# One of two feed-forward PSUM slots handed over bank by bank, a weight split moved behind the third residual addition, and a modulation step moved between two pieces

## The reference, cut to what matters

```python
def dwconv(x, w, b, left):
    K, L = w.shape[0], x.shape[1]
    xp = jnp.pad(x, ((0, 0), (left, K - 1 - left), (0, 0)))
    y = b + w[0] * xp[:, 0:L]
    for k in range(1, K):
        y = y + w[k] * xp[:, k:k + L]
    return y

def conv_ffn(z, w_up, conv_w, conv_b, w_down):
    u = dwconv(z @ w_up, conv_w, conv_b, FFN_CONV // 2)      # FFN_CONV = 3
    g, v = jnp.split(u, 2, axis=-1)
    return (jax.nn.silu(g) * v) @ w_down

# in each layer, for the latent and (in layer 0) the context tokens
mods = jnp.split((silu_c @ mod_w[l] + mod_b[l])[:, None, :], 6, axis=-1)
zl = modulate(rmsnorm(xl, norm2_g[l]), mods[3], mods[4])
xl = xl + mods[5] * conv_ffn(zl, ffn_w_up[l], ffn_conv_w[l], ffn_conv_b[l], ffn_w_down[l])
```

## Time and profile before

| | us |
|---|---|
| median of 3 runs | 3413.1 |
| lowest and highest | 3412.96, 3415.61 |
| the profiled execution's own time | 3416.35 |
| its span, first to last instruction | 3414.8 |
| TensorE matmuls busy | 3175.5 (93%) |
| VectorE busy | 1546.9 (45%) |
| ScalarE busy | 1020.6 (30%) |
| GpSimd busy | 310.6 (9%) |
| granted TensorE clock, mean over the span | 0.967 |

### The profile page before, as it was taken

One profiled execution on the slowest core, in us unless ns is written; L12 is line 12 of the kernel. 1 busy time (PEld: TensorE's weight loads), 2 busy tenths in 40 slices (PEclk: granted clock), 3 DMA queues, 4 the chain that ended last, 5 costly groups with the idle time before them and its releaser, 6 DMA issues. The chain is left out here.

```text
span 3414.8 us, 41073 instructions
## 1 busy us (share of the span) xinstructions
PE 3175.5 (93%) x17183; PEld 2547.1 (75%) x17183; DVE 1546.9 (45%) x1887; ACT 1020.6 (30%) x1190; POOL 310.6 (9%) x332
## 2 busy tenths in 40 slices
PE   4699799869899999999998999999989999999997
PEld 2566566558788888888886888888867787888786
DVE  3553544432544444444446533333343545444445
ACT  2344434421311111111113433333342322122212
POOL 1000000042000000000003322222211000000002
PEclk7899899989999999999999999999999999999998
DMA  7212220161221111111111011111031111111111
GB/s 268 59 47 76 66 70 33 40 238 54 68 74 62 56 61 52 60 62 60 59 62 55 24 44 48 37 37 36 24 118 44 50 50 48 39 56 44 50 44 50
DMA packets 197366, 215.28 MB, mean 63 GB/s; under 512 B 15538, under 2 KB 172327, under 8 KB 191045
## 3 DMA queue, kind: packets, MB, share of 16 engines
q1 hardware_dynamic: 187861, 160.12, 15.0%
q0 software_dynamic: 9328, 52.59, 4.5%
HBM read 190.27 MB, written 26.34 MB: 63 GB/s over the span
## 5 line engine op out<-in xcount | busy, mean ns | idle before, releaser
L747 PE MATMUL ps<-zH,wH 128*128 128x512 f32 (+1 forms) x2160 | 583.5, 370 | 46.6 <-DVE wL L943 43.4
L747 PE MATMUL ps<-zL,wH 128*128 128x512 f32 (+1 forms) x2160 | 579.6, 368 | 0.0
L747 PE MATMUL ps<-zH,wL 128*128 128x512 f32 (+1 forms) x2160 | 579.4, 368 | 0.0
L747 PEld LDWEIGHTS ps<-zH,wH 128*128 128x128 f32 x2160 | 375.3, 189 | 130.3 <-DVE wL L943 44.5
L747 PEld LDWEIGHTS ps<-zL,wH 128*128 128x128 f32 x2160 | 374.5, 188 | 70.6
L747 PEld LDWEIGHTS ps<-zH,wL 128*128 128x128 f32 x2160 | 374.5, 188 | 70.6
L1555 DVE SCALAR_TENSOR_TENSOR res<-ps,mod,res 128x1024 f32<-128x1024 f32 x240 | 236.6, 1014 | 210.3 <-PE ps L747 210.3
L757 DVE SCALAR_TENSOR_TENSOR V<-ps,vec,V 128x1023 f32<-128x1023 f32 (+1 forms) x132 | 134.1, 1016 | 391.2 <-ACT V L1432 388.0
L1408 ACT ACTIVATE wH<-wraw 128x1024 fp32r<-128x1024 f32 x130 | 134.5, 1049 | 419.4 <-PE ps L747 419.4
L757 DVE SCALAR_TENSOR_TENSOR G<-ps,vec,G 128x1023 f32<-128x1023 f32 (+1 forms) x132 | 134.1, 1016 | 234.2 <-ACT G L1432 231.0
L747 PE MATMUL ps<-hH,wH 128*128 128x512 f32 (+1 forms) x800 | 220.3, 373 | 20.3 <-DVEq L1534 20.3
(11 more groups left out here) (239 smaller groups left out, 4279.2 us busy)
## 6 DMA issues: line engine op xcount, KB each, us to landing
wraw<-in_ffn_w_up_dram SPq DMA_DIRECT2D x88, 512.0 KB, 3.8
modw<-in_mod_w_dram POOLq DMA_DIRECT2D x40, 1024.0 KB, 5.1
wraw<-in_ffn_w_down_dram SPq DMA_DIRECT2D x44, 512.0 KB, 3.7
wraw<-in_na_w_in_dram SPq DMA_DIRECT2D x24, 512.0 KB, 4.7
wraw<-in_rg_w_in_dram SPq DMA_DIRECT2D x20, 512.0 KB, 4.9
modring<-in_mod_w_dram SPq DMA_DIRECT2D x8, 1024.0 KB, 14.7
bias<-scratch_bias SPq DMA_DIRECT2D x32, 224.0 KB, 4.1
scratch_yT<-TR POOLq DMA_DIRECT2D x10, 640.0 KB, 3.2
```

The source lines that it names most:

```text
L747: last = nc.tensor.matmul(ps[:, slot * SLOT + c:slot * SLOT + c + n], w(k), r(k)[:, c:c + n], start=(k == 0 and i == 0), stop=(k == K - 1 ...
```

## The change

It has three parts, all in `ffn`.

1. In body groups the taps of gate 0 are made bank by bank (both taps of 512 columns, then a no-op that counts `bank_free`, then the next bank), and output unit 1, which writes the same slot, is computed bank by bank as well, waiting for `bank_free` ahead of each bank and no longer for `psum_free[0]`.
2. On VectorE the weight split that stood behind those taps (block 3 of the group, the weight of value 0) now stands behind the third residual addition.
3. Modulation step 0 moves from behind `first_pair` into it: between the gate unit and the value unit of piece 1.

```diff
@@ tensor, first_pair @@
                     if c == norm.n - 1:
                         ins.then_inc(unit_done, 1)
+                    if with_mod and (c, u) == (1, 0):
+                        modulation(0)
@@ tensor, group @@
             if first:
                 first_pair()
                 if with_mod:
-                    modulation(0)
                     modulation(1)
...
                     for mt in range(KD):
                         s = u % 2
+                        if mt == 1:
+                            by_bank(i, slot(first, k), slot(first, k + 1))
+                            u += 1
+                            continue
                         pe.wait_ge(psum_free[s], free(first, i, u))
...
+        def by_bank(i, s0, s1):
+
+            for c, (at, n) in enumerate(banks):
+                pe.wait_ge(bank_free, len(banks) * (i - 1) + c + 1)
+                for k, s in enumerate((s0, s1)):
+                    wH, wL = m.wH[:, s, P:2 * P], m.wL[:, s, P:2 * P]
+                    for q, (w, h) in enumerate(((wH, m.hH), (wH, m.hL), (wL, m.hH))):
+                        ins = nc.tensor.matmul(ps[:, at:at + n], w, h[:, k, at:at + n], start=(k == 0 and q == 0), stop=(k == 1 and q == 2))
+            ins.then_inc(unit_done, 1)
@@ vector, group @@
-                    taps(nc, dve, order, dst, src, [(-1, fcol(m, l, 0, col)), (1, fcol(m, l, 2, col))], ntok)
+                    if part_ is BODY and (kind, j) == ("g", 0):
+                        taps_by_bank(order, dst, col)
+                    else:
+                        taps(nc, dve, order, dst, src, [(-1, fcol(m, l, 0, col)), (1, fcol(m, l, 2, col))], ntok)
                     dve.nop().then_inc(psum_free[s], 1)
                     dve.nop().then_inc(g_conv if kind == "g" else v_conv, 1)
...
-                    after(first, i, b0, k + 3)
+                    if not (part_ is BODY and (kind, j) == ("g", 0)):
+                        after(first, i, b0, k + 3)
...
                         ins.then_inc(psum_free[s], 1)
                         u += 1
+                        if mt == 2:
+                            after(first, i, b0, k + 2)
...
+        def taps_by_bank(order, dst, col):
+
+            for c, n in banks:
+                for shift, w in ((-1, fcol(m, l, 0, col)), (1, fcol(m, l, 2, col))):
+                    seg = 0 if c < SEQ else SEQ
+                    end = min(SEQ, ntok) if c < SEQ else ntok
+                    lo, hi = max(seg, c - shift), min(end, c + n - shift)
+                    ins = nc.vector.scalar_tensor_tensor(out=dst[:, lo:hi], in0=ps[:, lo + shift:hi + shift], scalar=w, in1=dst[:, lo:hi],
+                                                         op0=ALU.mult, op1=ALU.add)
+                    order(ins)
+                dve.nop().then_inc(bank_free, 1)
```

More of the change, by code:

```diff
@@ L1229, in ffn @@
     assert 4 + 2 * (NG - 1) == MOD_STEPS
+    banks = chunks(ntok)
+    bank_free = sem(tag + "bank_free")
     def program(eng, group):
@@ L1524, in group @@
             k = u = 0
-            order = Order(dve, taps_order, 4 * (2 * ns) * i)
+            order = Order(dve, taps_order, 4 * (2 * ns) * i + (2 * (len(banks) - ns) * (i - 1) if i else 0))
             for kind, j in part_:
```

## The result

The changed kernel takes 3392.25 us (median of six, 3390.09 to 3394.12) where the kernel before takes 3413.53 beside it (six, 3410.5 to 3415.61): a ratio of 0.9938, 95% interval 0.9925 to 0.995. Forecast were 3392.0 and a range of 3388.5 to 3398.

The account below looks back on a forecast made before the run. It took TensorE as the bound, its matmuls busy for 93% of the span. Gains of 8.3 + 6.0 + 6.8 = 21.1 us, taken off the median of 3413.1, gave 3392.0 us, range 3388.5 to 3398.

Parts of the forecast that it names:

- First net, 8.3 us: First feed-forward net: the wait before output unit 1 goes whole, gaining 0.83 us a group, 8.3 us in ten.
- it just fits: First net: the first residual addition ends at 1048.70, before output unit 2 would start at 1048.88.
- Second net, 6.0 us: Second feed-forward net: bank-by-bank taps and output unit 1 gain 0.60 us a group, 6.0 us in ten.
- The split, nothing: VectorE: the weight split moved behind the third residual addition lies in idle time and costs nothing.
- The step, 6.8 us: First pair: modulation step 0 between pieces replaces the 5.55 us weight wait by one of about 1.5; gain 6.8 us.
- The sum, 21.1 us: Whole kernel: first net 8.3, second net 6.0 and the modulation step 6.8 add up to 21.1 us gained.
- B: Rival: the clock falls in the first pair, behind a thin step and 1.5 us idle; 3395 us, chance 0.15.
- C: Rival: VectorE's serial chain is longer than charged; second net gains 0.3 a group or less; 3397 us, chance 0.11.
- D: Rival: three short waits in place of one pull the clock down in the groups; 3448 us, chance 0.03.
- E: Rival: in both nets the waits move whole to the next release, only part 3 gains; 3406 us, chance 0.04.
- F: Rival: the no-ops overlap and the gain is 0.9 us a group in both nets; 3388 us, chance 0.05.
- The addition, and not the bank, is what is late next: Second net: output unit 2 waits for the first residual addition, ending 2766.98, while bank 1 is done at 2766.91.

Follow-up runs that it names:

- the four signals: The changed kernel with four signalling VectorE no-ops added between the taps of gate 0 and the first residual addition: 3403.28 us, ratio 0.9968.
- the run with sixteen signals: The changed kernel with sixteen signalling VectorE no-ops added between the taps of gate 0 and the first residual addition: 3427.36 us, ratio 1.0041.

## Why the prediction was right, point by point

**The bound.** It named one wait in each of twenty groups and one for the modulation weight. Those are the waits that went or, in the second net, became short, and the gain came from these places.

**First net, 8.3 us.** Measured 7.7 (0.76 a group in most, not 0.83). The wait went whole, and unit 2 starts 4.56 us behind the modulation step, as good as the 4.59 forecast. The small rest is the slower start that unit 2 pays there (0.10), which the sum charged in the second net only. It comes from the term of the no-ops: the first addition starts 0.41 us behind the taps, I charged 0.33, and "it just fits" became "just late". With the no-ops off the path unit 2 has no slower start and the period is 86.73; the four signals show that there is no slack at that place.

**Second net, 6.0 us.** Measured 4.7 (0.47 a group, forecast 0.60). The mechanism stood: bank 0's wait 0.21 us (by the sum's own times 2763.80 - 2763.59 = 0.21; the list of signs put it at about 0.35), taps of 3.22 us as worked out, and the residual addition as what is late next. The mis-sized terms are again the 0.33 for three no-ops (0.41) and the 0.02 between the addition's end and TensorE's start, which was 0.06 in the changed kernel (2814.88 + 1.28 = 2816.16 to 2816.22).

**The split, nothing.** Right: alone it moved no period. Left in place it cost 1.07 us a group, and the whole gain with it.

**The step, 6.8 us.** The stretch with steps 0 and 1 became 7.9 us shorter; less the step inserted ahead of it (1.15 forecast, 1.27 in like traces) that is 6.7. The wait that takes the place of the 5.55 us was forecast at 1.5 and is 1.40. How much the old arrangement cost depended on the clock: the stretch lasted 57.97 and 58.03 us in two traces, but 56.58 in the run with the split alone, where the clock came back sooner, so 5.3 would be the gain against that one.

**The sum, 21.1 us.** By the marks it is 7.7 + 4.7 + 6.7 = 19.1. The medians say 21.3, with the interval of the ratio 17 to 26. That the median came out 0.25 us from the forecast is in part luck: the terms were 2.0 us too large together.

**The rivals.** B did not occur: the clock was 1.00 behind the first pair. What spoke for it was read from a single execution. The lower clock behind the wait of 1.2 us at L664 came in three of twelve traces; the changed kernel had the same wait and the same thin matmuls at the upper level, and its clock fell some 10 us later (two windows of the changed kernel, columns as in the earlier trace rows):

```profile
859.00:862.00 3.00, 2.93 (x25) 2.94 (x26) 2.70 (x6) 1.61 (x4) 0.00 (x0) 1.00 0.00 0
870.00:876.00 6.00, 5.32 (x12) 3.75 (x13) 5.65 (x10) 2.68 (x4) 0.00 (x0) 0.50 0.31 90
```

C's mechanism is real, since the chain on VectorE is somewhat longer than charged, but it took 0.13 a group, not 0.3. D did not occur in the changed kernel. The row that the prediction cites for the clock after the wait of 1.27 us, 2763 to 2764, ends before that wait does; the windows over the groups show what was meant, first the second net before, then both nets of the changed kernel:

```profile
2700.00:3340.00 640.00, 628.53 (x2763) 517.54 (x2762) 308.88 (x249) 139.11 (x131) 0.00 (x0) 1.00 0.15 46
```

```profile
920.00:1780.00 860.00, 860.00 (x4442) 712.55 (x4442) 405.55 (x443) 163.22 (x138) 11.72 (x21) 1.00 0.19 62
2680.00:3320.00 640.00, 637.71 (x2777) 519.18 (x2777) 316.29 (x271) 140.79 (x133) 0.00 (x0) 1.00 0.15 46
```

What the Trainium skill's rule ("TensorE: Matmul & The Clock Gate", section "A second HAM failure mode: psum-queue depth-cycling") describes was seen in one group of the run with sixteen signals only, behind a wait of 1.82 us. E is ruled out by the periods. F would have needed no-ops that cost nothing; taking them off the path gave what F had put at 0.9 a group (0.88 in both nets by the periods of 86.73 and 65.97).

**"The addition, and not the bank, is what is late next"** was the sentence on which most hung, and three runs bear it out: with the split ahead of the addition both periods grow by 1.07, with four more signals ahead of it by 0.38, and with none of them TensorE goes faster. In that last run the bank is what unit 2 follows: the addition has ended at 2749.80, and unit 2 starts at 2750.04 without a slower start, right behind bank 1.

## What to carry to other kernels

Before splitting a hand-over into parts, write out what the releasing engine does next, to the last no-op, up to the release after this one: here the finer hand-over was worth nothing until the work behind it was moved too. A single buffer that is used twice in a row puts its load on the path (a wait of 5.55 us here); put other work between the uses, and count what the inserted work delays. Where a bank or two are free, a unit with banks of its own is better than a finer wait (65.39 against 65.97 us a group, both without no-ops on the path).

## What the runs showed of the hardware

**A signalling no-op on VectorE costs 0.09 to 0.13 us** where the next operation is on the path: 0.38 us for three, 0.11 for one between taps, 0.095 each for four more. Waiting for a count that the operations raise anyway costs none of it.

**Where the clock falls differs from one execution to the next, for the same instructions and the same waits.** The stretch from gate 1 of the last group to the end is not touched by the change. It has the same counts of operations in both profiled executions (in brackets), yet the mean granted clock was 0.83 in that of the kernel before and 0.89 in that of the changed one, and it lasted 74.0 and 70.6 us:

```profile
3340.82:3414.80 73.98, 54.30 (x244) 45.35 (x242) 38.14 (x51) 22.17 (x32) 18.01 (x14) 0.83 0.14 57
```

```profile
3319.37:3390.00 70.63, 50.39 (x244) 41.52 (x242) 38.24 (x51) 22.19 (x32) 18.03 (x14) 0.89 0.15 60
```

In all twelve traces it lasted 70.6 to 74.3, and the stretch between the two nets' groups 851.5 to 856.2. In the first pair the fall came at one of three places, as the table above has it. Such differences are as large as the terms of this sum. They are why single profiled times should not be subtracted to size a change of some microseconds, and why the periods of repeated groups were used here.

**Open.** In the runs with four and sixteen signals, some groups are 0.35 to 0.4 us longer than the others. The chain of waits of the second shows a stretch of 0.4 us among the no-ops in which VectorE waits for nothing recorded; in one group of the first it stands at the no-op between two banks, where the next tap starts 0.50 us behind the one before, not 0.15. What that is, no run here tells apart.
